# Second mixer's scores: fp32 matmuls of unsplit queries and keys in place of three fp32r passes

## The chip, the cores and the metric

One core of a Trainium2 chip runs the kernel. The metric is the device time of one execution in microseconds. Engines: PE is TensorE (PEld its weight loads), DVE is VectorE, ACT is ScalarE, POOL is GpSimd, SP issues the DMAs of the weights.

## The reference

A decoder trunk of two layers on 512 tokens of width 1024, in float32. Layer 0 mixes tokens with a mixture of dilated attentions, layer 1 with differential attention; each layer then has a squared-ReLU MLP (width 4096) and a gated per-layer input. The change touches layer 1's attention alone: 8 heads, each with two halves of 64 dimensions, causal in blocks of 128 queries:

```python
q = q.reshape(B, T, HEADS_B, 2, HEAD_DIM)
k = k.reshape(B, T, HEADS_B, 2, HEAD_DIM)
logits = jnp.einsum('bqhje,bkhje->bhjqk', qblk, k,
                    preferred_element_type=jnp.float32) * scale + bias
logits = jnp.where(dist >= 0, logits, -jnp.inf)
probs = jax.nn.softmax(logits, axis=-1)
attn = probs[:, :, 0] - lam * probs[:, :, 1]
```

## The kernel before

Activations lie transposed in SBUF: 128 partitions of channels, 512 tokens along the free dimension. Every matrix product is made from two fp32r parts of each operand: the high part (a copy into an fp32r tile) and the low part (the difference). `passes` (L1597) issues three matmuls, high by high (L1599), low by high (L1600), high by low (L1601). A unit is one 128-column slab of a weight matrix against all 512 tokens: 8 chunks, 24 passes of 128x512, in one PSUM bank. Each unit's weights come by one DMA into `w_raw`, ScalarE makes `w_hi` (L845), VectorE `w_lo` (L1140).

The second mixer runs in steps (`b_steps`), one head behind the other. In step s three units are projected, Q, K and V of head s (`B_ORDER`), and the scores of head s - 1 are made in three items (`B_BLOCKS`): item 0 is query block 3 against 512 keys, item 1 block 2 against 384, item 2 block 1 against 256 and block 0 against 128. The order on TensorE within an item (`sub_b` of the tensor block) is: the scores of this item, the transposes of the item before, a projection unit, and the values' matmuls (L1980) of the item before. Steps 2 to 7 are a loop of three rounds; two more steps drain, with units of the output projection beside them. Every engine has its own program in program order; semaphores join them.

VectorE scales each unit's bank into SBUF at L1466 (`out_of`, which counts evac_done). Q and K go to two slabs of `h_a` (`b_product`), V to another. Before, ScalarE copies Q and K to an fp32r high part (`split_qk_hi`, L884, called at L1064), and VectorE subtracts for the low part (`split_qk_lo`, L1150, called at L1511), counting qk_ready. `b_parts` names where the parts lie: the high part in slots of `qk_hi`, which lies over `heads`, the low part in `qk_lo_b`, which lies over the first four slabs of `h_a`. The scores of one block:

```python
for j in range(2):
    rows = slice(j * E, (j + 1) * E)
    last = passes(logits[:, j * T + first:j * T + first + keys],
                  (q_hi[rows, tile], q_lo[rows, tile]),
                  k_hi[rows, 0:keys], k_lo[rows, 0:keys], True, True)
```

The two halves j use partitions 0 to 63 and 64 to 127 and write different banks of `logits`. The weights of these matmuls are the queries' 64x128, the keys stream. VectorE then adds the bias (L1478), ScalarE makes the exponentials (L1058).

Three other places of the kernel already multiply unsplit fp32 tiles: the first mixer's scores for two of its groups (L1723, in `scores_a`: 64x128 by 64x128, 8 matmuls in each of two banks in a step, the halves j alternating), the values of both mixers (L1741, L1980), and the column sums of the norms (L1670, in `statistics`: 128 rows, 512 columns, called five times).

Of the kernel before, what the change touches and what calls it, by code (L numbers as in the profile page):

```python
# [38 lines left out]
P = 128  # L39
T = 512  # L40
# [196 lines left out]
def build(nc, x, p, rel_bias, a_w_qkv, a_w_o, b_w_qkv, b_w_o, lq1, lk1, lq2, lk2, subln, norm_mix,  # L237
          norm_mlp, w_ff1, w_ff2, norm_ple, w_gate, w_proj, final_norm, selector, out):
    ctx = ExitStack()
    with ctx:  # L240
# [13 lines left out]
        act1_lo = sb("act1_lo", [P, KC, T], F32R)  # L254
        act0_hi = sb("act0_hi", [P, KC, T], F32R)
        act0_lo = sb("act0_lo", [P, KC, T], F32R)

        with nc.sbuf_tensor("qk_lo_b", [P, 4, T], F32R) as qk_lo_b:
            pass
        h_a = sb("h_a", [P, KC, T])  # L260
        w_raw = [sb(f"w_raw{i}", [P, KC + KP, P]) for i in range(2)]
        w_hi = [sb(f"w_hi{i}", [P, KC + KP, P], F32R) for i in range(2)]
# [166 lines left out]
        def b_v_t(par):  # L429

            return h_a[:, KC // 2 + par, :]

        def b_product(i):

            return h_a[:, KC - 2 + i, :]

        def a_segments(ph):


# [51 lines left out]
        def b_buf(par, kind):  # L491
            o = KC * T + (par * 3 + kind) * T
            return heads[:, o:o + T]

        def b_parts(par, kind):

            o = KC * T + (par * 3 + kind) * T
            return qk_hi[:, o:o + T], qk_lo_b[:, 2 * par + kind, :]

        s_small = sem("s_small")  # L500
        s_table = sem("s_table")
# [330 lines left out]
        def _(sc):  # L832
# [209 lines left out]
            def sub_b(s, par, i, has_proj, has_scores, has_prev, has_norm):  # L1042
                u = s.times(B_UNITS) + U_B
                t = (s - 1).times(B_ITEMS) + (ITEMS_A + i)
                early = [] if has_proj else b_drain(s, i)
                next_hi(u + i if has_proj else early[0])
                if s.reg is None and s.const == 0 and i == 1:
                    statistics(3)
                if has_prev:
                    keys = b_width((i - 1) % B_ITEMS)  # L1050
                    wait(sc, turned_ready, t)
                    sc.activation(probs_t[:, 0:keys], turned[:, 0:keys], ACT.Copy).then_inc(pt_a_ready, 1)
                if has_scores:
                    wait(sc, logits_done, t + 1)
                    for _, first, keys, col in b_blocks(i):
                        for j in range(2):
                            cols = slice(j * T + first, j * T + first + keys)
                            e = sc.activation(probs[i][:, cols], probs[i][:, cols], ACT.Exp,  # L1058
                                              bias=low[:, col + j:col + j + 1], scale=-1.0,
                                              accum_out=total[:, col + j:col + j + 1])  # L1060
                    e.then_inc(exp_done, 1)
                if has_proj and i > 0:

                    split_qk_hi(b_parts(par, B_ORDER[i - 1]), b_product(i - 1), u + i)  # L1064
                if has_scores and i == 0:
                    wait(sc, vt_ps, s + A_PAIRS)
                    sc.activation(b_buf(1 - par, V), misc[:, :], ACT.Copy).then_inc(v_ready, 1)
                if has_norm and i == 1:
                    wait(sc, o_clamped, s - 1)
                    for a in range(NT):  # L1070
                        block = square[1][:, a * P:(a + 1) * P]
                        last = sc.activation(block, block, ACT.Square, scale=SHRINK,
                                             accum_out=head_sum[:, a:a + 1])
                    last.then_inc(osq_ready, 1)
                    wait(sc, osq_ready, s - 1)
                    sc.activation(head_root[:, :], head_sum[:, :], ACT.Sqrt, scale=1.0 / P,
                                  bias=eps_col[:, 1:2]).then_inc(oroot_ready, 1)

                    sc.activation(spare[:, :], eps_col[:, 0:1], ACT.Exp)
                if has_norm and i == 2:  # L1080
                    wait(sc, oturned_ps, s - 1)
                    sc.activation(MID[1][0][:, bass.ds((s - 2).v, 1), :], flat3(misc), ACT.Copy,
                                  scale=sub_gain[:, :]).then_inc(o_hi_ready, 1)
                for e_unit in early[1:]:
                    next_hi(e_unit)
# [47 lines left out]
        def _(ve):  # L1133
# [322 lines left out]
            def sub_b(s, par, i, has_proj, has_scores, has_prev, has_norm):  # L1456
# [4 lines left out]
                pr = probs[i]  # L1461

                def out_of(unit_at, kind, to):
                    dst = b_v_t(to) if kind == V else b_product(B_ORDER.index(kind))
                    wait(ve, units_done, unit_at + 1)
                    ve.tensor_tensor(dst, bank_of(unit_at)[:, :], (rstd_q if kind == Q else rstd)[:, :],  # L1466
                                     ALU.mult).then_inc(evac_done, 1)
# [25 lines left out]
                if has_scores:  # L1493
# [13 lines left out]
                        last = ve.scalar_tensor_tensor(both, both, inv[:, col - 2 * i:col - 2 * i + 1],  # L1507
                                                       pr[:, T + first:T + first + keys], ALU.mult, ALU.subtract)
                    last.then_inc(probs_ready, 1)
                if has_proj and i > 0:  # L1510
                    split_qk_lo(b_parts(par, B_ORDER[i - 1]), b_product(i - 1),  # L1511
                                s.times(2) + (2 * A_PAIRS + i))
                for n, e_unit in enumerate(early):
                    if n:
                        next_lo(e_unit)
# [80 lines left out]
        def _(te):  # L1596
# [325 lines left out]
            def sub_b(s, par, i, has_proj, has_scores, has_prev, has_norm):  # L1922
                u = s.times(B_UNITS) + U_B
                t = (s - 1).times(B_ITEMS) + (ITEMS_A + i)
                if has_scores:
                    if i == 0:
                        wait(te, qk_ready, s.times(2) + 2 * A_PAIRS)
                    wait(te, logits_done, t)
                    (q_hi, q_lo), (k_hi, k_lo) = b_parts(1 - par, Q), b_parts(1 - par, K)
                    for block_q, first, keys, _ in b_blocks(i):  # L1930
                        tile = slice(block_q * P, (block_q + 1) * P)
                        for j in range(2):
                            rows = slice(j * E, (j + 1) * E)
                            last = passes(logits[:, j * T + first:j * T + first + keys],
                                          (q_hi[rows, tile], q_lo[rows, tile]),
                                          k_hi[rows, 0:keys], k_lo[rows, 0:keys], True, True)
                    last.then_inc(scores_ready, 1)

                prev = (i - 1) % B_ITEMS
                prev_par = 1 - par if i else par  # L1940
                tiles = [(block_q, c, first + c * P) for block_q, first, _, _ in b_blocks(prev)
                         for c in range(block_q + 1)]
                if has_prev:
                    wait(te, probs_ready, t)
                    turn(turned, [(col, probs[prev][:, col:col + P]) for _, _, col in tiles]
                         ).then_inc(turned_ready, 1)
                turns_head = has_norm and i == 2
                if has_proj:

                    opening = s.reg is None and s.const == 0 and i == 0  # L1950
                    if turns_head:
                        unit(u + i, IN[1], part=(0, KC // 2))
                        turn_head(s)
                        unit(u + i, IN[1], part=(KC // 2, KC)).then_inc(units_done, 1)
                    else:
                        whole(u + i, IN[1], act_ready if opening else None, 3 * KC)
                    if opening:
                        statistics(3)
                else:
                    for n, e_unit in enumerate(b_drain(s, i)):  # L1960
                        if turns_head and n == 0:
                            out_early(e_unit, 1, (0, 3))
                            turn_head(s)
                            out_early(e_unit, 1, (3, KC - LATE[1]))
                        else:
                            out_early(e_unit, 1)
                if has_scores and i == 0:


                    wait(te, evac_done, s.times(B_UNITS) + U_B)  # L1970
                    turn(misc, [(a * P, b_v_t(1 - par)[:, a * P:(a + 1) * P])
                                for a in range(NT)]).then_inc(vt_ps, 1)
                if has_prev:
                    if i == 1:
                        wait(te, v_ready, s + A_PAIRS)
                    wait(te, pt_a_ready, t)
                    if has_norm and i == 1:
                        wait(te, o_copied, s - 1)
                    for block_q, c, col in tiles:
                        last = te.matmul(attn[:, block_q * P:(block_q + 1) * P], probs_t[:, col:col + P],  # L1980
                                         b_buf(prev_par, V)[:, c * P:(c + 1) * P], start=c == 0,
                                         stop=c == block_q)
                    last.then_inc(pv_done, 1)
# [69 lines left out]
```

## Time and profile before

| | us |
|---|---|
| median of 3 timed runs | 1618.43 (1618.02 to 1618.88) |
| the profiled execution | 1616.87 |
| its span in the trace | 1615.1 |
| TensorE busy | 1598.4 (99%), granted clock 0.998 |
| VectorE busy | 906.1 (56%) |
| ScalarE busy | 606.3 (38%) |

A row of the trace's timeline gives the start, the duration, the engine, the line, the operation, its tiles and shapes, and how many equal neighbours it merges. A matmul's duration contains its latency and overlaps the next, so cost is read from start to start. A matmul of fp32 tiles is recorded as more than one instruction. The second mixer lies between about 960 and 1178 us, its scores between 976.6 and 1154.

### The profile page before, as it was taken

The numbers are of one execution on the slowest core, as the hardware profiler recorded it, in microseconds if no ns is written. First come the engines' busy times: TensorE is split into PE (matmuls) and PEld (weight loads), VectorE is DVE, ScalarE is ACT, GpSimd is POOL, SyncE is SP. The second block draws the span as 40 slices with busy tenths as digits, with TensorE's granted clock in tenths as the row PEclk, the third lists the DMA queues.
The fourth block names the chain that finished last, engine by engine and source line by source line (L and its number), as shares of the span: only waits on it lengthen the run. The fifth ranks groups of instructions, "written<-read, shape, count | busy, mean of one in ns | idle before, by whom it ended". The sixth has DMA issues, their size and how long they took to land.

```text
span 1615.1 us, 22040 instructions
## 1 busy us (share of the span) xinstructions
PE 1598.4 (99%) x8243; PEld 1319.5 (82%) x8243; DVE 906.1 (56%) x1589; ACT 606.3 (38%) x1090; POOL 61.1 (4%) x60
## 2 busy tenths in 40 slices
PE   8999999999999999999999999999999999999998
PEld 7888888888888788888888878888878888888887
DVE  5364455555555863635455676777676363535555
ACT  5233333334334431222223444766652132212344
POOL 0000000000000200000001110000020000000111
PEclk9999999999999999999999999999999999999999
DMA  6533443443332333333333333323233333333331
GB/s 161 157 111 93 118 115 91 112 122 84 99 88 69 105 91 97 96 96 93 100 91 103 99 103 100 92 74 95 66 92 98 99 91 104 91 102 93 92 113 70
DMA packets 300571, 160.12 MB, mean 99 GB/s; under 512 B 31545, under 2 KB 295282, under 8 KB 300514
## 3 DMA queue, kind: packets, MB, share of 16 engines
q1 hardware_dynamic: 300112, 158.61, 34.7%
q0 software_dynamic: 144, 0.71, 0.2%
q8 instruction: 37, 0.61, 0.2%
q14 instruction: 20, 0.16, 0.0%
q10 hardware_dynamic: 258, 0.04, 0.0%
HBM read 157.11 MB, written 10.60 MB: 104 GB/s over the span
## 4 chain that ended last, share of the span: by engine, by line
PE 95%; POOL 1%; DVE 1%; ACT 1%; DMA 1%; issue 0%; ACTq 0%; POOLq 0%; SPq 0%
PE unit_out L1599 26%; PE unit_out L1601 26%; PE unit_out L1600 26%; PE turned L1675 2%; PE attn L1741 2%; POOL sumsq L827 1%; PE attn L1980 1%; PE unit_out L1760 1%; PE logits L1675 1%; PE unit_out L1761 1%; PE unit_out L1762 1%; PE logits L1599 1%; PE misc L1675 1%; PE misc L1599 1%; PE misc L1601 1%; PE misc L1600 1%
## 5 line engine op out<-in xcount | busy, mean ns | idle before, releaser
L1599 PE MATMUL unit_out<-act_hi,w_hi 128*128 128x512 f32 x1857 | 730.6, 393 | 2.7 <-DVE w_lo L1140 1.8
L1601 PE MATMUL unit_out<-act_hi,w_lo 128*128 128x512 f32 x1857 | 721.9, 389 | 0.0
L1600 PE MATMUL unit_out<-act_lo,w_hi 128*128 128x512 f32 x1857 | 721.1, 388 | 0.0
L845 ACT ACTIVATE w_hi<-w_raw 128x1024 fp32r<-128x1024 f32 (+3 forms) x257 | 272.1, 1059 | 461.4 <-PE unit_out L1601 350.4
L1599 PEld LDWEIGHTS unit_out<-act_hi,w_hi 128*128 128x128 f32 x1857 | 348.7, 188 | 77.9 <-DVE w_lo L1140 4.6
L1601 PEld LDWEIGHTS unit_out<-act_hi,w_lo 128*128 128x128 f32 x1857 | 348.6, 188 | 73.2
L1600 PEld LDWEIGHTS unit_out<-act_lo,w_hi 128*128 128x128 f32 x1857 | 349.0, 188 | 70.1 <-issue 0.7
L1140 DVE TENSOR_TENSOR w_lo<-w_raw,w_hi 128x1024 fp32r<-128x1024 f32 (+3 forms) x257 | 321.4, 1251 | 118.1 <-ACT w_hi L845 118.0
L1004 ACT ACTIVATE act_hi<-hidden 128x512 fp32r<-128x512 f32 x64 | 40.5, 633 | 243.4 <-DVE hidden L1400 243.4
L827 POOL TENSOR_TENSOR sumsq<-sumsq,square 128x512 f32<-128x512 f32 x41 | 57.8, 1410 | 1527.8 <-ACT square L873 1526.1
L1397 DVE TENSOR_TENSOR scaled<-unit_out,rstd 128x512 f32<-128x512 f32 x62 | 42.8, 690 | 67.7 <-PE unit_out L1601 67.7
L1220 DVE TENSOR_TENSOR h_a<-h_a,unit_out 128x512 f32<-128x512 f32 x39 | 26.8, 687 | 90.0 <-PE unit_out L1601 90.0
L1220 DVE TENSOR_TENSOR heads<-heads,unit_out 128x512 f32<-128x512 f32 x40 | 27.5, 686 | 84.1 <-PE unit_out L1601 84.1
L943 ACT ACTIVATE probs<-probs,w_raw 128x256 f32<-128x256 f32 (+1 forms) x128 | 61.8, 484 | 32.6 <-DVE w_raw L1244 32.6
L1403 DVE TENSOR_TENSOR act_lo<-hidden,act_hi 128x512 fp32r<-128x512 f32 x64 | 44.3, 692 | 44.7 <-ACT act_hi L1004 44.7
L1400 DVE SCALAR_TENSOR_TENSOR hidden<-scaled 128x512 f32<-128x512 f32 x64 | 44.3, 692 | 2.2
L1478 DVE CUSTOM_DVE_ANT_0 probs<-logits,bias 128x512 f32<-128x512 f32 (+3 forms) x64 | 28.2, 487 | 25.9 <-PE logits L1601 25.9
L1058 ACT ACTIVATE probs<-probs,low 128x512 f32<-128x512 f32 (+3 forms) x64 | 35.4, 553 | 7.4 <-DVE low L1478 7.4
L860 ACT ACTIVATE act_hi<-heads,gains 128x512 fp32r<-128x512 f32 x24 | 17.3, 722 | 49.1 <-DVE heads L1220 25.6
L1312 DVE TENSOR_TENSOR act_lo<-attn,act_hi 128x512 f32 (+1 forms) x8 | 5.5, 691 | 53.6 <-ACT act_hi L957 53.6
L1229 DVE TENSOR_SCALAR probs<-probs,w_raw 128x256 f32<-128x256 f32 (+1 forms) x128 | 35.2, 339 | 0.3
L1244 DVE CUSTOM_DVE_ANT_0 probs<-logits,bias 128x256 f32<-128x256 f32 (+1 forms) x64 | 21.1, 386 | 20.4 <-PE logits L1723 20.4
(275 smaller groups left out, 1392.4 us busy)
## 6 DMA issues: line engine op xcount, KB each, us to landing
w_raw<-in_w_ff_dram SPq DMA_DIRECT2D x128, 512.0 KB, 4.0
w_raw<-in_a_w_qkv_dram SPq DMA_DIRECT2D x56, 512.0 KB, 3.9
w_raw<-in_b_w_qkv_dram SPq DMA_DIRECT2D x24, 512.0 KB, 5.1
w_raw<-in_a_w_qkv_dram SPq DMA_DIRECT2D x32, 256.0 KB, 3.1
w_raw<-in_w_ple_gate_dram SPq DMA_DIRECT2D x16, 512.0 KB, 4.0
bias_tiles_b<-bias_vectors SPq DMA_DIRECT2D x16, 256.0 KB, 4.2
bias<-bias_tiles_b SPq DMA_DIRECT2D x8, 512.0 KB, 3.7
w_raw<-in_a_w_o_dram SPq DMA_DIRECT2D x8, 448.0 KB, 3.7
```

The lines of the kernel that those rows point to most:

```text
L827: pool.tensor_tensor(sumsq[:, :], sumsq[:, :], square[n % 2][:, :], ALU.add).then_inc(sumsq_done, 1)
L845: sc.activation(weights_of(u)[0][:, 0:width, :], w_raw[par][:, 0:width, :], ACT.Copy).then_inc(hi_done, 1)
L943: e = sc.activation(probs[i][:, cols], probs[i][:, cols], ACT.Exp, bias=low_col, scale=-1.0, accum_out=sum_col)
L1140: ve.tensor_tensor(lo[:, 0:width, :], w_raw[par][:, 0:width, :], hi[:, 0:width, :], ALU.subtract).then_inc(lo_done, 1)
L1220: ve.tensor_tensor(h[:, n, :], h[:, n, :], unit_out[u.const % 2][:, :], ALU.add).then_inc(evac_done, 1)
L1397: ve.tensor_tensor(scaled[:, :], bank_of(u)[:, :], rstd[:, :], ALU.mult).then_inc(evac_done, 1)
L1400: ve.scalar_tensor_tensor(hidden[:, :], scaled[:, :], 0.0, scaled[:, :], ALU.max, ALU.mult).then_inc(hid_ready, 1)
L1403: ve.tensor_tensor(MID[layer][1][:, n, :], hidden[:, :], MID[layer][0][:, n, :], ALU.subtract).then_inc(hid_done, 1)
L1599: te.matmul(bank, w_k[0], hi, start=start, stop=False)
L1600: te.matmul(bank, w_k[0], lo, start=False, stop=False)
L1601: return te.matmul(bank, w_k[1], hi, start=False, stop=stop)
L1675: last = te.transpose(bank[:, dst:dst + P], src, ident[:, :])
```

## The change

The queries and keys are written once, as fp32, into `b_buf` slots of `heads`; both parts, `b_parts`, `b_product`, `qk_lo_b` and the calls of the two splits in the second mixer are gone. A block is one fp32 matmul for each half. The first scores of a head wait for the evacuation of the K unit in place of the second subtraction. The first mixer is untouched.

```diff
-        with nc.sbuf_tensor("qk_lo_b", [P, 4, T], F32R) as qk_lo_b:
-            pass
...
-        def b_product(i):
-
-            return h_a[:, KC - 2 + i, :]
-
...
-        def b_parts(par, kind):
-
-            o = KC * T + (par * 3 + kind) * T
-            return qk_hi[:, o:o + T], qk_lo_b[:, 2 * par + kind, :]
...
-                if has_proj and i > 0:
-
-                    split_qk_hi(b_parts(par, B_ORDER[i - 1]), b_product(i - 1), u + i)
...
-                    dst = b_v_t(to) if kind == V else b_product(B_ORDER.index(kind))
+                    dst = b_v_t(to) if kind == V else b_buf(to, kind)
...
-                if has_proj and i > 0:
-                    split_qk_lo(b_parts(par, B_ORDER[i - 1]), b_product(i - 1),
-                                s.times(2) + (2 * A_PAIRS + i))
...
-                        wait(te, qk_ready, s.times(2) + 2 * A_PAIRS)
+                        wait(te, evac_done, s.times(B_UNITS) + (U_B - 1))
                     wait(te, logits_done, t)
-                    (q_hi, q_lo), (k_hi, k_lo) = b_parts(1 - par, Q), b_parts(1 - par, K)
+                    q, k = b_buf(1 - par, Q), b_buf(1 - par, K)
                     for block_q, first, keys, _ in b_blocks(i):
                         tile = slice(block_q * P, (block_q + 1) * P)
                         for j in range(2):
                             rows = slice(j * E, (j + 1) * E)
-                            last = passes(logits[:, j * T + first:j * T + first + keys],
-                                          (q_hi[rows, tile], q_lo[rows, tile]),
-                                          k_hi[rows, 0:keys], k_lo[rows, 0:keys], True, True)
+                            last = te.matmul(logits[:, j * T + first:j * T + first + keys],
+                                             q[rows, tile], k[rows, 0:keys], start=True, stop=True)
```

## Rows read from the trace of the kernel before

**Rows 1.** The page: busy time and share of each engine; the chain by engine.
```profile
PE 1598.4 (99%) x8243; PEld 1319.5 (82%) x8243; DVE 906.1 (56%) x1589; ACT 606.3 (38%) x1090; POOL 61.1 (4%) x60
PE 95%; POOL 1%; DVE 1%; ACT 1%; DMA 1%; issue 0%; ACTq 0%; POOLq 0%; SPq 0%
```
**Rows 2.** Longest wait of TensorE's weight loads, 977 to 1160 us (us, times, longest).
```profile
PEld turned L1675 <- issue: 4.5, 15, 0.4
...
```
**Rows 3.** Busy time in one window (clock after POOL); timelines around 1012 us.
```profile
1000.00:1150.00 150.00, 150.00 (x852) 123.67 (x851) 108.65 (x263) 98.83 (x240) 0.00 (x0) 1.00 0.29 81
...
1011.83 0.68 DVE L1150 TENSOR_TENSOR qk_lo_b<-h_a,qk_hi 128x512 fp32r<-128x512 f32 x1
...
1011.85 0.39 PE L1601 MATMUL unit_out<-act_hi,w_lo 128*128 128x512 f32 x1
1012.08 0.39 PE L1599 MATMUL unit_out<-act_hi,w_hi 128*128 128x512 f32 x1
```
**Rows 4.** Splits of the second mixer by line, then VectorE's timeline.
```profile
L884 ACT ACTIVATE qk_hi<-h_a 128x512 fp32r<-128x512 f32 x16 | 9.9, 619 | 5.0 <-DVE h_a L1466 5.0
L1150 DVE TENSOR_TENSOR qk_lo_b<-h_a,qk_hi 128x512 fp32r<-128x512 f32 x16 | 11.0, 685 | 0.7 <-ACT qk_hi L884 0.7
...
996.98 0.69 DVE L1150 TENSOR_TENSOR qk_lo_b<-h_a,qk_hi 128x512 fp32r<-128x512 f32 x1
999.89 0.69 DVE L1478 CUSTOM_DVE_ANT_0 probs<-logits,bias 128x512 f32<-128x512 f32 x1 [2.23 <-PE logits L1601]
```
**Rows 5.** Timeline of TensorE around the three score items of one head.
```profile
998.76 0.50 PE L1599 MATMUL logits<-qk_hi 64*128 64x512 f32 x2
999.10 0.39 PE L1600 MATMUL logits<-qk_lo_b,qk_hi 64*128 64x512 f32 x2
999.33 0.39 PE L1601 MATMUL logits<-qk_hi,qk_lo_b 64*128 64x512 f32 x2
999.65 0.55 PE L1675 MATMUL turned<-ident,probs 128*128 128x128 f32 x3
...
1006.72 0.45 PE L1599 MATMUL logits<-qk_hi 64*128 64x384 f32 x2
1007.00 0.34 PE L1600 MATMUL logits<-qk_lo_b,qk_hi 64*128 64x384 f32 x2
1007.18 0.34 PE L1601 MATMUL logits<-qk_hi,qk_lo_b 64*128 64x384 f32 x2
1007.46 0.66 PE L1675 MATMUL turned<-ident,probs 128*128 128x128 f32 x4
...
1014.42 0.39 PE L1599 MATMUL logits<-qk_hi 64*128 64x256 f32 x2
...
1015.26 0.55 PE L1675 MATMUL turned<-ident,probs 128*128 128x128 f32 x3
```
**Rows 6.** The scores' matmuls by line and their widths.
```profile
L1599 PE MATMUL logits<-qk_hi x64: 217/410/494, 976.6 to 1153.7; 64*128 64x512 f32 x16, 64*128 64x384 f32 x16, 64*128 64x256 f32 x16, 64*128 64x128 f32 x16
```
**Rows 7.** Timeline of the first mixer's fp32 scores in one step.
```profile
80.56 1.16 PE L1723 MATMUL logits<-heads 64*128 64x128 f32 x16
81.56 1.06 PE L1723 MATMUL turned<-heads 64*128 64x128 f32 x16
82.55 0.50 PE L1760 MATMUL unit_out<-w_hi,act_hi 128*128 128x512 f32 x1
```
**Rows 8.** The statistics' fp32 matmul, 512 columns: records and timeline of one.
```profile
L1670 PE MATMUL attn<-sumsq,ones x10: 590/592/697, 557.2 to 1553.0; 128*128 128x512 f32 x10
...
1201.81 0.70 PE L1670 MATMUL attn<-sumsq,ones 128*128 128x512 f32 x1 [0.17 <-POOL sumsq L827]
...
1202.35 0.59 PE L1670 MATMUL attn<-sumsq,ones 128*128 128x512 f32 x1
1202.89 0.50 PE L1599 MATMUL unit_out<-act_hi,w_hi 128*128 128x512 f32 x1
```
**Rows 9.** Timeline behind the second mixer: the copy that opens the stall.
```profile
1177.91 1.06 ACT L845 ACTIVATE w_hi<-w_raw 128x1024 fp32r<-128x1024 f32 x1 [1.46 <-PE unit_out L1601]
```

## The prediction

> **What bounds the kernel now.** I read the page from the top. TensorE is busy 99% of the span, 1598.4 of 1615.1 us, and the chain that ended last is 95% TensorE [rows 1]. Since a modelled matmul end overlaps the next start, "busy" alone proves little, so the second view is the list of waits in the second mixer's steady stretch, 977 to 1160 us. TensorE's own list is empty, and its weight loads show 15 short "issue" gaps ahead of the transposes, two single ones elsewhere, and no wait for another engine [rows 2]. The third view is the timeline: projection passes of 512 columns start every 0.23 us, at a granted clock of 1.00 [rows 3]. So in this stage a microsecond counts only if TensorE issues it. VectorE and ScalarE have slack: of 150 us they are busy 108.65 and 98.83 [rows 3].
>
> **What goes from ScalarE and VectorE.** 16 splits to the high part at 0.62 us (9.9 us busy) and 16 subtractions at 0.69 us (11.0 us) disappear; the splits' source, the products at L1466, stay at the same size and change only their place in SBUF [rows 4]. I cost this at nothing, because TensorE waits for neither engine here [rows 2]. The cover would be gone only if TensorE waited for them. Can it give something through less contention? The passes beside L1150 (1011.83, for 0.68 us) start at 1011.85 and 1012.08, 0.23 us apart [rows 3], and so do passes of the same width while VectorE idles, 999.10 and 999.33 [rows 4, 5]. I take 0 and keep 0.3 us of gain as the lower bound. No DMA is issued by the removed code, and none is moved.
>
> **The wait that changes.** TensorE's first scores of a head waited for both subtractions (qk_ready) and will wait for the K product alone (evac_done). That is strictly earlier in VectorE's order: the subtraction comes after it. The last one before the scores at 998.76 began at 996.98 and lasted 0.69 us, so it was over about 1.1 us ahead [rows 4]. I cost it at nothing.
>
> **What the split scores cost now.** Per head there are three items: one 512-wide block, one of 384, and one with 256 and 128. Each block has three passes for each of two halves of 64 rows. The timeline shows them in pairs: L1599 x2, then L1600 x2, then L1601 x2 [rows 5], although the code issues all three passes of one half before those of the other. So the two halves run side by side on the two halves of the array, and a block costs three steps, not six. From the first start to the first start of the next instruction: 998.76 to 999.65 = 0.89 us, 1006.72 to 1007.46 = 0.73 or 0.74 us (0.73 is used), 1014.42 to 1015.26 = 0.84 us [rows 5]; 2.46 us a head, 19.7 us for eight. The counts of 16 in each width (8 heads, 2 halves) say that all heads are alike [rows 6]. In these times: a step of 512 is 0.23 us (999.10 to 999.33), of 384 0.175, of 256 0.115; 0.89 less three steps leaves 0.21 us for filling and draining around the group, split evenly into 0.11 (the first step of 0.34 less 0.23) and 0.10 [rows 5].
>
> **What the fp32 scores will cost.** The trace has two kinds of unsplit fp32 matmuls that answer this. First, the number of passes: the first mixer's scores at L1723 are fp32 and 128 wide; the code issues 8 into each of two banks in a step, the trace records 16 in each [rows 7], so one fp32 matmul is two passes. The statistics at L1670 say the same: 5 in the code, 10 recorded [rows 8]. Second, the time of a pass: for 512 columns on 128 rows the starts are 1201.81, 1202.35 and (next instruction) 1202.89, 0.54 us each [rows 8]. Less 0.11 us of filling in the first and about as much draining in the second, a pass of 512 is 0.43 us, or 0.84 ns a column; the fp32r pass is 0.45 ns a column. Third, whether halves of 64 rows pair: 32 records at L1723 take 80.56 to 82.55 = 1.99 us [rows 7]; less 0.21 us that is 0.11 us for each pair of passes of 128 columns, 0.87 ns a column. In sequence, 32 passes at 0.11 us would have taken 3.5 us. So pairing works for fp32 too, in the order of halves that the change uses.
>
> Thus a block is two steps of 0.84 ns a column where it was three of about 0.45:
> - 512: 0.21 + 2 x 0.43 = 1.07 us against 0.89, +0.18 (L1670's two intervals give 1.08 directly);
> - 384: 0.21 + 2 x 0.32 = 0.86 (0.855) against 0.73, +0.125;
> - 256 and 128: 0.21 + 2 x 0.215 + 2 x 0.11 = 0.86 against 0.84, +0.02. The three split steps of 128 columns were not bound by their columns: 0.84 less 0.21 and 3 x 0.115 leaves 0.285 us for them, where 0.45 ns a column makes 0.17. The fp32 steps lose no such time, so this item comes out nearly even.
>
> Sum +0.33 us a head, +2.7 us for eight heads. Bounds of this term: with all the overhead taken out of the steps (0.833 ns a column, 0.10 us to drain) +2.3; with 15 ns of overhead on each fp32 pass (an fp32r step of 384 has as much: 0.175 us against 0.160 for 384 columns at 2.4 GHz) and 0.12 us to drain, +3.5.
>
> One rule of the Trainium skill speaks against the pairing. The records show the second half's L1599 ahead of the first half's L1600 [rows 5]. The Trainium skill (TensorE: Matmul & The Clock Gate, The mechanism) says that weight loads can be pulled forward but that matmuls start and end in strict program order. The trace does not agree: in strict order the split block of 512 would take five steps, 0.21 + 5 x 0.23 = 1.36 us, and it took 0.89 [rows 5].
>
> **What is late next.** Nothing takes over: VectorE's first read of the scores follows them by 0.24 us (999.65 to 999.89) [rows 4, 5] and shifts by under 0.2 us, with its slack above. The stall behind this mixer (a ScalarE copy at 1177.91 that TensorE's own unit releases [rows 9]) lies 24 us after the last score and moves with TensorE.
>
> **The rivals.**
> - *Halves in program order (slower).* Two passes of one half, then two of the other; only the neighbouring passes of different halves overlap, so three steps a block. 512: 0.21 + 3 x 0.43 = 1.50; 384: 0.21 + 3 x 0.32 = 1.17; the third item 0.21 + 3 x 0.215 + 2 x 0.11 = 1.08. Over 2.46 that is +1.29 a head, +10.3 us: 1628.7 us. It decides from the point at which a wider or longer fp32 pass stops the reordering. Against it: L1723 and the split blocks [rows 5, 7]; for it only that no wide fp32 pair exists. By the strict order that the Trainium skill states (the section named above) this would be the outcome. Chance 0.06.
> - *No pairing at all.* Four steps a block: 1.93 + 1.49 + 1.51 = 4.93, +2.47 a head, +19.8 us: 1638.2 us. Chance 0.02.
> - *A 64-row fp32 pass is as fast by the column as fp32r (faster).* The 0.11 us of L1723 could be a floor of the weight load and not the columns' time, since the split steps of 128 columns too took 0.095 us each, more than their columns need. Then 0.21 + 2 x 0.23 = 0.67, 0.56, and 0.21 + 2 x 0.115 + 2 x 0.11 = 0.66: 1.89, -0.57 a head, -4.6 us: 1613.8 us. Against it: L1670 at 512 columns [rows 8], which are of 128 rows, though. Chance 0.05.
> - *Overhead on wide fp32 passes*, beyond the forecast's steps: the upper bound above and a little more, +3.3 to +4.2 us, 1621.7 to 1622.6. Chance 0.17.
> - *The shorter list of work pays*: fewer instructions and a lighter ScalarE and VectorE turned into time: needs a wait of TensorE on them, and there is none [rows 2]. It would end at 1618.4 or a little below, within no change. Chance 0.05.
>
> **How the numbers follow.** The profiled execution took 1616.87 us, 1.8 us around its span; the sum gives 1619.6 for such a run. The median of the three timed runs is 1618.43, 1.6 us above, so the forecast is 1618.43 + 2.7 = 1621.1 us, chance 0.65. Its own range is 1620.0 to 1621.9 (the term from +2.3, less the 0.3 of contention, to +3.1, and runs that differ by 0.4). 0.2%, about what a measurement of this kernel can tell from no change, is 3.2 us: the bound is 1621.7, just above my value, so a tenth of the forecast's chance falls beyond it, with the overhead case and the two order rivals: slower 0.07 + 0.17 + 0.08 = 0.32. Faster: 0.05. Same: the rest, 0.63. The range from 1618.9 to 1622.9 leaves out both order rivals, the fast fp32 pass and the no-cost case, 0.18 in all.
>
> **What would show it.** In the profile after: 128 records of the scores into logits where there were 192; groups x4 for a block, from first start to the transposes 1.07, 0.86 and 0.86 us; no L884 and L1150 in this stage; VectorE and ScalarE 11.0 and 9.9 us less busy at an unchanged pace of the projection; the span +2.7 us. If a block of 512 takes 1.5 us, the order rival holds; if 0.67, a fp32 pass on 64 rows is cheap. A new wait of TensorE anywhere in 977 to 1160 us would make the reasoning wrong, whatever the sum.

## The result and the profile after

The changed kernel takes 1620.20 us (median of 20 runs), the kernel before 1617.84 us (20 runs beside it): +2.4 us, ratio 1.0014 with a 95% interval of 1.0008 to 1.0020. This is a slowdown that the runs can tell from zero, and it is at most 0.2%. The profiled execution took 1620.19 us with a span of 1618.4.

The page after (busy time of each engine), which answers [rows 1]; TensorE holds 95% of the chain, as before:

```profile
PE 1601.1 (99%) x8179; PEld 1315.2 (81%) x8179; DVE 896.4 (55%) x1573; ACT 598.5 (37%) x1074; POOL 61.1 (4%) x60
```

There are 64 matmul records fewer (192 became 128). VectorE is 9.7 us and ScalarE 7.8 us less busy, and TensorE 2.7 us more. So there are fewer instructions on all three engines, and the kernel is longer. The timeline of TensorE around the three score items of one head, against [rows 5]:

```profile
1000.03 1.13 PE L1916 MATMUL logits<-heads 64*128 64x512 f32 x4
1001.09 0.33 PE L1657 MATMUL turned<-ident,probs 128*128 128x128 f32 x1
...
1008.16 0.92 PE L1916 MATMUL logits<-heads 64*128 64x384 f32 x4
1009.01 0.33 PE L1657 MATMUL turned<-ident,probs 128*128 128x128 f32 x1
...
1015.97 0.92 PE L1916 MATMUL logits<-heads 64*128 64x256 f32 x8
1016.82 0.33 PE L1657 MATMUL turned<-ident,probs 128*128 128x128 f32 x1
```

A group is all score matmuls of one item; its time is read from its first start to the transposes' first start: 1.06, 0.85 and 0.85 us. In nanoseconds, as the medians of the eight heads, the groups went from 890, 732 and 836 to 1060, 846 and 854: +302 ns a head, +2.4 us for eight.

Does that account for the whole? Two column sums of the norms (the third and the fourth of five) stand before and behind the second mixer. Their starts in the kernel before, then after (the later one of before is in [rows 8]):

```profile
964.42 0.70 PE L1670 MATMUL attn<-sumsq,ones 128*128 128x512 f32 x1 [0.18 <-POOL sumsq L827]
...
965.34 0.70 PE L1652 MATMUL attn<-sumsq,ones 128*128 128x512 f32 x1 [0.19 <-POOL sumsq L815]
...
1205.16 0.70 PE L1652 MATMUL attn<-sumsq,ones 128*128 128x512 f32 x1 [0.18 <-POOL sumsq L815]
```

Between them lay 1201.81 - 964.42 = 237.39 us and now lie 1205.16 - 965.34 = 239.82 us: +2.43, the score groups' +2.4. The profiled spans differ by 3.3 us, because this execution was already 0.92 us late at the first of the two, in code that the change doesn't touch; behind the second both need 413.2 to 413.3 us. This stretch between two fixed points is the yardstick for the experiments. Each kernel's stretch is read from one execution. Less its 24 score groups it is 217.7 us here in both kernels, and between 217.4 and 217.9 us in those that follow, so a difference of 0.3 us in the stretch alone shows nothing; the groups themselves repeat within 14 ns from head to head.

TensorE's waits in 977 to 1163 us: its own list is again empty, and the weight loads' has "issue" alone (columns: us in all, times, longest), against [rows 2]:

```profile
PEld turned L1657 <- issue: 9.7, 15, 0.8
PEld unit_out L1581 <- issue: 0.8, 1, 0.8
...
```

Those 9.7 us look like a new wait, and aren't one. The loads of the 512-key block are over 0.30 us after its group's start, and the transposes' loads begin only with the transposes, 1.06 us after it; the gap of 0.76 us between them lies inside the time that the groups count already.

### The profile page after: what moved, and what is told of

It is laid out like the page before. It is cut to its first block, busy times and chain, and to the rows that moved or that the text cites. A ratio compares the mean times of both kernels' runs of the same rounds, so it can differ in the third digit from the quotient of the medians.

```text
span 1618.4 us, 21865 instructions
## 1 busy us (share of the span) xinstructions
PE 1601.1 (99%) x8179; PEld 1315.2 (81%) x8179; DVE 896.4 (55%) x1573; ACT 598.5 (37%) x1074; POOL 61.1 (4%) x60
## 4 chain that ended last, share of the span: by engine, by line
PE 95%; POOL 1%; DVE 1%; DMA 1%; ACT 1%; issue 0%; ACTq 0%; POOLq 0%; SPq 0%
PE unit_out L1581 26%; PE unit_out L1583 25%; PE unit_out L1582 25%; PE turned L1657 2%; PE attn L1723 2%; POOL sumsq L815 1%; PE logits L1916 1%; PE attn L1961 1%; PE unit_out L1742 1%; PE logits L1657 1%; PE unit_out L1743 1%; PE unit_out L1744 1%; PE misc L1657 1%; PE misc L1581 1%; PE misc L1583 1%; PE misc L1582 1%
```

## The experiments

**Theory.** In this mixer only TensorE's issue counts. A group costs a fixed 0.21 us, plus one step for each pair of passes (one pass of each half, side by side); a step costs by kind (fp32r or fp32) and column. **Rivals.** The relief of ScalarE and VectorE gave something back, so that the fp32 passes cost more than the net shows; the cost comes from changing kinds, not from columns; the halves pair only in a suitable order.

### The changed kernel again, as the yardstick

> The changed kernel beside the three that follow, as their yardstick. Both theories: +2.4 us on the kernel before (the score groups took 1.060, 0.846 and 0.854 us a head against 0.890, 0.732 and 0.836: +0.30 us a head, eight heads).

Measured: 1620.78 us against 1617.80, ratio 1.0017 (1.0008 to 1.0026); the groups of 1060, 846 and 854 ns, the stretch between the column sums 239.85 us. As expected.

### The splits kept alive

```diff
-        def b_product(i):
+        def b_product(par, i):
-            return h_a[:, KC - 2 + i, :]
+            o = (14 + 2 * par + i) * T
+            return heads[:, o:o + T]
...
+                            if block_q in (0, 1, 2, 3):
+                                last = te.matmul(logits[...], b_product(1 - par, 0)[rows, tile],
+                                                 b_product(1 - par, 1)[rows, 0:keys], start=True, stop=True)
+                                continue
                             last = passes(...)
```

The diff is against the kernel before; the calls of both splits and the old wait stay, and `passes` is reached by no block.

> Scores of all four blocks directly in fp32, but ScalarE and VectorE still make the high and low parts, which nothing reads, and the old wait for them stays; the products lie in four slabs of heads of their own. Theory (TensorE alone sets the pace, the splits were hidden): the same as the changed kernel, +2.4 us on the kernel before, groups of 1.06, 0.85 and 0.85 us. Rival (the lighter ScalarE and VectorE, or the earlier release, gave something back, so that the fp32 passes really cost more than +2.4): clearly slower than the changed kernel; had the removed 21 us of their work been worth even a tenth, +4.5 us on the kernel before.

Measured: 1620.68 us, 1.0016 (1.0007 to 1.0025), beside 1620.78 for the changed kernel on the same chip. The groups took 1060, 847 and 854 ns, the stretch 239.94 us against 239.85. The work is there again (lines of the second mixer, columns as in [rows 4]):

```profile
L1151 DVE TENSOR_TENSOR qk_lo_b<-heads,qk_hi 128x512 fp32r<-128x512 f32 x16 | 11.0, 687 | 0.7 <-ACT qk_hi L885 0.7
L885 ACT ACTIVATE qk_hi<-heads 128x512 fp32r<-128x512 f32 x16 | 9.9, 618 | 5.0 <-DVE heads L1467 5.0
```

20.9 us of work on two engines, and the old wait with it, change the median by -0.1 us and the stretch by +0.1: less than either resolves (the changed kernel's own runs lie up to 2.1 us apart, 1619.70 to 1621.84). The rival's own figure, +4.5 us on the kernel before, is excluded by the interval of +1.1 to +4.0 us. A gain of a few tenths of a microsecond is not excluded.

### One block at a time

Both use the kernel above with another condition, `if block_q in (3,)` for the 512-key block or `(0,)` for the 128-key block; the other blocks keep their split passes.

> Only the block of 512 keys directly in fp32, the other three with split parts as before; splits kept. Theory (cost by column: two paired steps of 0.427 us for three of 0.227): its group 1.06 us against 0.89, the other two at 0.73 and 0.84; +0.17 us a head, +1.4 us in all. Rival (the cost is a change of kind between fp32r and fp32, one for each group): +0.8 us, a third of 2.4.

> Only the block of 128 keys directly in fp32, the other three with split parts; splits kept. Theory (a step of 128 columns has a floor of about 0.1 us whatever its kind, so two steps beat three): third group 0.78 us against 0.836, the others as before; -0.06 us a head, -0.45 us in all, too little for the timed runs but plain in the trace. Rival (switching kinds inside a group costs an emptying of the array, 0.1 us or more): third group 0.88 us or longer, +0.4 us in all.

Measured, 512 alone: 1619.48 us, 1.0010 (1.0000 to 1.0019). Groups 1060, 732 and 836 ns, so the block itself added 170 ns a head, 1.36 us; the stretch is 238.53 us, +1.14. The timed +1.7 us agrees within its interval, and so would the rival's 0.8. It is the groups that decide: 1.06 us, where a fixed price of changing kinds (0.8 us over eight heads, 0.1 us a head) would make 0.99.

Measured, 128 alone: 1617.25 us, 0.9995 (0.9986 to 1.0004), not resolved by the timed runs. The third group:

```profile
1015.05 0.39 PE L1600 MATMUL logits<-qk_hi 64*128 64x256 f32 x2
...
1015.39 0.29 PE L1602 MATMUL logits<-qk_hi,qk_lo_b 64*128 64x256 f32 x2
1015.50 0.39 PE L1936 MATMUL logits<-heads 64*128 64x128 f32 x4
1015.83 0.33 PE L1676 MATMUL turned<-ident,probs 128*128 128x128 f32 x1
```

1015.83 - 1015.05 = 0.78 us, as expected, and fp32r and fp32 stand side by side in it without an empty place between 1015.39 and 1015.50. The direct form is cheaper at 128 columns (0.779 us for this group against 0.836) and dearer from 256 on: with the 256-key block in fp32 too the group takes 0.854 us, 75 ns more. Two things were not expected. This kernel's 512 group, whose code is that of before, took 900 ns in place of 890; one of the eight heads of before took 904 as well. And the stretch, 236.64 us, is 0.75 us shorter where the groups give 0.42. Both are open.

### The order of issue, split passes

```diff
-                        for j in range(2):
-                            rows = slice(j * E, (j + 1) * E)
-                            last = passes(...)
+                        for n, (a, b) in enumerate(((q_hi, k_hi), (q_lo, k_hi), (q_hi, k_lo))):
+                            for j in range(2):
+                                rows = slice(j * E, (j + 1) * E)
+                                last = te.matmul(logits[...], a[rows, tile], b[rows, 0:keys],
+                                                 start=n == 0, stop=n == 2)
```

> The kernel before with its split passes issued in another order: for each of the three passes the first half, then the second. Theory (the two halves run in pairs whatever order they are issued in): no change, groups of 0.89, 0.73 and 0.84 us. Rival (the order counts and the pairs seen in the trace are only how it is drawn): if strict order held for the kernel before, five steps a block would fall to three, -0.45 us for 512 columns and some -8 us in all.

Measured: 1617.42 us against 1617.97, 0.9995 (0.9986 to 1.0005); groups 890, 725 and 829 ns, the stretch 237.17 us, 0.2 us less than before. In the 512 group, issued in turn, the halves start 3 ns apart where they started 10 ns apart, and that is all that the order bought. So the kernel before already ran its halves in pairs, although three passes of the first stand ahead of the second's first. With strict order as the cost of before, this kernel would have been some 8 us faster; strict order falls.

### How far the pairing reaches

Three kernels issue the third item half by half, with the loop over the halves outside that over the blocks. The second half's first pass then stands four passes behind the first half's (the changed kernel), five (the kernel with the 128-key block alone in fp32) or six (the kernel before):

```diff
-                    for block_q, first, keys, _ in b_blocks(i):
-                        for j in range(2):
+                    for j in range(2):
+                        for block_q, first, keys, _ in b_blocks(i):
```

> The changed kernel with the third item issued half by half: four passes of the first half (256 twice, 128 twice), then four of the second. Theory (halves pair out of issue order): the third group stays at 0.854 us, no change on the changed kernel, +2.4 us on the kernel before. Rival (strict order, pairs only between neighbours): only one pass of each half overlaps, 0.21 + 4 x 0.215 + 3 x 0.11 = 1.40 us, +4.4 us on the changed kernel, +6.8 us on the kernel before.

> The kernel before with its third item issued half by half: six passes of the first half (256 three times, 128 three times), then six of the second. Theory (the second half is taken forward over at least six passes): third group 0.84 us as before. Rival (the reach is shorter than six passes and their weight loads): a group of 1.0 us or more, with records of the first half alone at its head.

> The kernel with the 128-key block alone in fp32, its third item issued half by half: five passes of the first half (three split ones of 256, two fp32 ones of 128), then five of the second. The second half kept pace over four passes and not over six. Theory (its fifth pass ahead is still taken forward): third group 0.78 us, as with the blocks in turn. Rival (the reach ends at four): the second half's first pass starts one pass late, 0.22 us behind the first half's, and the group takes 0.95 us or more.

Measured, four passes: 1620.24 us against 1617.97, 1.0016 (1.0006 to 1.0026), the third group 861 ns against 854. The pairs hold. The other two kernels were each run once, six passes at 1621.03 us and five at 1618.34, which is too few to compare times; their traces decide, and in each all eight heads agree within 3 ns. Six passes: the third group took 1184 ns, the theory falls and its rival stands:

```profile
1016.39 0.38 PE L1599 MATMUL logits<-qk_hi 64*128 64x256 f32 x1
...
1016.73 0.27 PE L1601 MATMUL logits<-qk_hi,qk_lo_b 64*128 64x256 f32 x1
1016.73 0.38 PE L1599 MATMUL logits<-qk_hi 64*128 64x256 f32 x2
...
1017.57 0.33 PE L1675 MATMUL turned<-ident,probs 128*128 128x128 f32 x1
```

The second half's L1599 starts at 1016.73, together with the first half's third pass. The stretch is 239.99 us, +2.6, with nothing changed but the order of issue. With five passes between them the theory falls too: the second half joins with the first half's second pass (1015.26 and 1015.27), and the group takes 1001 ns, not 780:

```profile
1015.04 0.38 PE L1600 MATMUL logits<-qk_hi 64*128 64x256 f32 x1
1015.26 0.28 PE L1601 MATMUL logits<-qk_lo_b,qk_hi 64*128 64x256 f32 x1
1015.27 0.38 PE L1600 MATMUL logits<-qk_hi 64*128 64x256 f32 x1
...
1016.04 0.44 PE L1676 MATMUL turned<-ident,probs 128*128 128x128 f32 x2
```

Four ahead: paired from the start; five: from the second pass; six: from the third. In these kernels a pass to free rows of the array is taken forward over up to four passes, no further. The unit is the recorded pass and not the column or the matmul in the code. By columns, three passes of 512 (1536 columns) are overtaken in the kernel before, and five with 1024 are not. By matmuls in the code, where an fp32 one is two passes, the two late kernels would disagree: three overtaken with five passes, four with six. The late start is the whole price: the second half begins 0.23 and 0.35 us behind the first in place of 0.01, and the group is 0.22 and 0.35 us longer (1001 ns for 779, 1184 for 836).

### No pairing

The diff is against the changed kernel. Both halves read the first 64 rows; the second half's queries and keys are left out.

```diff
-                            rows = slice(j * E, (j + 1) * E)
+                            rows = slice(0, E)
```

> The changed kernel with both halves reading partitions 0 to 63, so that the second softmax is made of the first half's queries and keys; the number and size of matmuls are the same, but the two cannot lie side by side in the array. Theory: four steps a block in place of two: 0.21 + 4 x 0.427 = 1.92, 0.21 + 4 x 0.32 = 1.49 and 0.21 + 4 x 0.213 + 4 x 0.107 = 1.49 us; 4.90 against 2.76 a head, +17 us on the changed kernel, +19.5 us on the kernel before. Rival (pairing gives nothing, a pass of fp32 on 64 rows takes 0.21 us of its own): no change on the changed kernel.

Measured: 1637.17 us, 1.0116 (1.0100 to 1.0133), +19.2 us on the kernel before. The 512 group:

```profile
1001.82 1.98 PE L1916 MATMUL logits<-heads 64*128 64x512 f32 x4
1003.73 0.33 PE L1657 MATMUL turned<-ident,probs 128*128 128x128 f32 x1
```

1.91 us, and 1.485 and 1.50 us for the others, as by four steps a block; the rival, no change, falls. Pairing is worth 17 us of this kernel, seven times what the change moved.

### One pass

The diff is against the changed kernel. Queries and keys are written as fp32r and multiplied once; their low parts are left out.

```diff
-            return heads[:, o:o + T]
+            return heads[:, o:o + T] if kind == V else qk_hi[:, o:o + T]
```

> The changed kernel with queries and keys written as fp32r and multiplied once: the low parts are left out, one paired step a block. Theory (a step costs by kind and column: fp32r 0.227 us for 512, 0.175 for 384, 0.117 for 256, about 0.11 for 128): groups of 0.21 + 0.227 = 0.44, 0.385 and 0.21 + 0.117 + 0.11 = 0.44 us; 1.26 a head against 2.46, -1.2, or -9.6 us on the kernel before and -12 us on the changed kernel. Rival (VectorE and ScalarE, which read scores only after them, become the bound once the scores are short): a gain clearly below 9 us, with TensorE waiting for one of them.

Measured: 1608.12 us against 1617.97, 0.9935 (0.9919 to 0.9952), -9.9 us; groups 430, 377 and 378 ns, the stretch 226.99 us, -10.4. Of the third group:

```profile
1013.97 0.45 PE L1916 MATMUL logits<-qk_hi 64*128 64x256 f32 x4
1014.35 0.33 PE L1657 MATMUL turned<-ident,probs 128*128 128x128 f32 x1
```

The expectation missed here by 0.06 us a head (0.378 us for 0.44): a single step of 128 columns behind one of 256 costs about 0.06 us, near what its columns need, and not 0.11. The floor of 0.1 us shows only where several steps of 128 follow each other. With scores this short TensorE's list of waits in this stage is still empty, so no other engine becomes the bound even 10 us lower.

### The small gains together

This is the kernel before with its split passes issued alternately and the 128-key block alone in fp32. The expectation's "first to fourth column sum" is the stretch from the third to the fourth.

> The two small gains together: split passes issued alternating between the halves, and the block of 128 keys directly in fp32. From the traces of the two alone (score groups -0.12 us and -0.42 us in all; first to fourth column sum 237.17 and 236.64 us against 237.39): score groups -0.55 us, the stretch between the column sums between 236.4 and 236.6 us, -0.8 to -1.0 us on the kernel before. Rival (each of these differences is chance of one execution): the stretch lies back at 237.2 to 237.5 us and the timed runs show nothing.

Measured: 1617.15 us against 1617.97, 0.9994 (0.9985 to 1.0003). Groups 893, 722 and 772 ns, the stretch 236.46 us, -0.9. The expectation of the stretch was met. Its groups are 0.58 us shorter than those of the kernel before in all; the other 0.35 us is of the size by which the rest of the stretch differs from kernel to kernel. The timed interval includes no change, so the kernel isn't shown to be faster.

## Why the prediction was right

**What bounds the kernel.** Right: in 977 to 1150 us TensorE's list of waits stayed empty in every kernel run, with the scores at 10 us less as with the splits kept.

**The splits at nothing.** Right as far as the runs resolve, by the kernel that keeps them: 0.1 us for 20.9 us of work, by the medians and by the stretch. The wait that moved was worth nothing to be seen either, since that kernel keeps the old one. The sign "11.0 and 9.9 us less busy" came at 9.7 and 7.8 on the page. The removed instructions are the ones that were named, and the durations summed over all instructions fell by 11.0 and 9.8 us; the page counts time in which two instructions of an engine overlap once.

**Steps and passes.** Right: two steps for three, in pairs. The sum had the groups at 1.07, 0.86 (0.855) and 0.86 us, and they took 1.060, 0.846 and 0.854. The split groups were read from one head, 0.89, 0.73 and 0.84; the median third one is 0.836. The term came out at +2.4 where +2.7 stood. Of that 0.3 us, 0.1 is an error of the sum: 0.18 + 0.125 + 0.02 is 0.325 us a head, 2.6 us for eight. The rest is 10 ns each on the 512 and 384 groups, from times read to two digits (a step is 0.427 us and not 0.43). The bounds of the term don't come out of their own numbers either: 0.833 ns a column and 0.21 us around a group make 1.06, 0.85 and 0.85 us, +2.4 and not +2.3, and the upper case makes +3.9 and not +3.5. The measured term is the lower bound as redone: no overhead on the passes is to be seen.

**The median.** 1621.1 was forecast and 1620.2 measured. 0.3 us of that is the term; the other 0.6 us is the kernel before, which moved from 1618.43 with three runs to 1617.84 with twenty. The two errors go the same way, so neither hid the other.

**The rivals.** *Halves in program order* was priced at +10.3 us and didn't come. Its point was left as "a wider or longer fp32 pass", and that was the wrong quantity: what decides in these kernels is how many passes of one half stand ahead of the other's, at most four. The change has two, and the kernel before three. *No pairing* was priced at +19.8 us and measured, with the rows made equal, at +19.2. *A 64-row fp32 pass as fast as fp32r* fell at 512 columns (two steps of 0.427). Its premise, a floor under steps of 128 columns, is real: in the kernel before, the weight loads of the third item start 0.11 us apart (1014.53, 1014.65, 1014.76, 1014.88, 1014.98), and so do its later steps of 128, which fits with the 128-key block alone being cheaper in fp32. That the loads set the floor isn't tested by any run. *Overhead on wide passes* fell: two wide steps cost 0.85 us, which is four times 512 columns at 2.4 GHz with nothing to spare. *The shorter list of work pays* fell: the kernel is slower by the groups' 2.4 us, and with the splits kept it takes the same.

## What to carry to other kernels

Where TensorE alone sets the pace, count the columns of its steps by kind and not the instructions: dropping two splits and a third of the passes cost time, since an fp32 pass needs 0.83 ns a column where an fp32r pass needs 0.45, and two of the one exceed three of the other from 256 columns on. Matmuls on 64 rows are worth laying out so that the two halves pair, by these traces within four passes of each other; this was worth seven times the change. And before an engine's relief is counted as a gain, look whether anyone waits for it.

## What the runs showed of the hardware beyond the forecast

- TensorE starts matmuls out of the order of issue when they use other rows of the array, over up to four passes: paired from the start at four, from the second pass at five (group of 1001 ns against 779 with the blocks in turn), from the third at six (1184 ns against 836). The Trainium skill (TensorE: Matmul & The Clock Gate, The mechanism) has matmuls start in strict program order; these traces don't agree.
- A change between fp32r and fp32 within a group costs nothing to be seen: 1015.39 to 1015.50, 0.11 us from the last split step of 256 columns to the first fp32 step, as between two split steps of that width.
- An fp32 matmul of 512 columns takes 2 x 0.427 = 0.853 us at a granted clock of 1.00: two records, and four times 512 columns at 2.4 GHz.
- A lone step of 128 columns costs about 0.06 us (one pass), a row of them 0.09 to 0.11 us each (the kernel before and the changed one).
